# A streaming-encoder layer on eight cores: the second block's attention gate projected ahead of its Q and K, with other staging of the last weights

## The reference, cut to what matters

```python
x = layer_norm(x, ln0_g, ln0_b)
q, k, v, z_a, B, C, h, z_c = split(x @ w_in, 8)        # each 512 wide
y_att  = chunk_attention(q, k, v, rel_bias) * silu(z_a)  # 8 heads of 64, chunks of 64, 8 chunks back
y_conv = B * causal_depthwise_conv3(C * h) * silu(z_c)
hh = concat(y_att, y_conv) @ w_out
out = layer_norm(2 ** 0.25 * x + hh, ln_g, ln_b)
```

## Time and profile before

| what | before |
|---|---|
| median of 3 runs | 1300.98 us (1300.01 to 1301.29) |
| the profiled execution | 1299.6 us, span of its slowest core (core 6) 1298.1 us |
| spans of the cores | 1295.1 (cores 3 and 5) to 1298.1 us (core 6) |
| TensorE busy | 1255.1 us, 97% of the span |
| VectorE, ScalarE, GpSimd busy | 964.7, 742.5, 508.8 us |
| chain that ended last | PE 92%, DMA 3%, issue 2%, DVE 2% |

### The profile page before, as it was taken

How to read it: one execution, slowest core, us unless ns; L and a number is a source line. 1 busy time by engine, 2 the same in 40 slices (tenths; PEclk the granted TensorE clock), 3 DMA queues, 4 the chain that set the end, 5 groups by cost and what they waited for, 6 DMA issues and landing times.

```text
span 1298.1 us, 27186 instructions; the slowest of 8 cores (1295.1 to 1298.1 us)
## 1 busy us (share of the span) xinstructions
PE 1255.1 (97%) x8145; PEld 596.3 (46%) x8308; DVE 964.7 (74%) x1763; ACT 742.5 (57%) x1090; POOL 508.8 (39%) x768
## 2 busy tenths in 40 slices
PE   5989999999999999999999999999999999999996
PEld 3434444444444444444444444444444444444443
DVE  2479976878777686776867768787776867868487
ACT  5775565655536565565654546565564555656562
POOL 2455442533334342443533424434344323424242
PEclk9999999999999999999999999999999999999999
DMA  9993323312233322323213223123232223232022
GB/s 292 324 252 107 88 72 86 90 42 74 72 84 90 82 67 57 83 75 89 74 42 89 75 83 90 47 69 79 78 90 75 73 58 86 74 86 58 10 74 74
DMA packets 125712, 117.15 MB, mean 90 GB/s; under 512 B 103168, under 2 KB 103168, under 8 KB 125440
## 3 DMA queue, kind: packets, MB, share of 16 engines
q1 hardware_dynamic: 125568, 115.40, 32.3%
HBM read 57.69 MB, written 33.55 MB: 70 GB/s over the span
## 4 chain that ended last, share of the span: by engine, by line
PE 92%; DMA 3%; issue 2%; DVE 2%; ACT 1%; SPq 1%; POOL 0%; DVEq 0%; ACTq 0%; POOLq 0%
PE mm L673 32%; PE sc L673 16%; PE mm L684 13%; PE mm L787 12%; PE sc L1015 6%; PE sc L959 5%; PE sc L787 4%; PE sc L684 4%; DMA xs<-w_in 3%; PE sc L856 1%; DVE xs L617 0%; SPq L587 0%; ACT PT L972 0%; DVE xs L926 0%; DVE tz L744 0%
## 5 line engine op out<-in xcount | busy, mean ns | idle before, releaser
L673 PE MATMUL mm<-xnT,w_in_sb 128*128 128x512 bf16 x2002 | 491.9, 379 | 9.3 <-POOL w_in_sb L511 3.8
L972 ACT ACTIVATE PT<-sc 128x1024 bf16<-128x1024 f32 (+1 forms) x288 | 269.9, 1001 | 122.7 <-PE sc L959 121.9
L673 PEld LDWEIGHTS mm<-xnT,w_in_sb 128*128 128x128 bf16 x2072 | 195.3, 98 | 204.8 <-issue 20.1
L673 PE MATMUL sc<-xnT,w_in_sb 128*128 128x512 bf16 x971 | 242.3, 379 | 1.9 <-DVE tz L744 0.6
L1015 PE MATMUL sc<-vA,PT 128*128 128x65 bf16 x2240 | 203.2, 193 | 5.3 <-DVE PT L999 1.8
L1015 PEld LDWEIGHTS sc<-vA,PT 128*128 128x128 bf16 x2240 | 149.3, 97 | 109.3 <-issue 3.5
L1033 POOL TENSOR_TENSOR pvs<-pvs,rden 128x256 f32<-128x256 f32 x128 | 124.6, 974 | 154.6 <-DVE rden L1032 91.3
L999 DVE TENSOR_TENSOR PT<-PT,etab 128x512 bf16<-128x512 bf16 (+1 forms) x304 | 119.9, 404 | 87.4 <-ACT PT L972 83.3
L684 PE MATMUL mm<-w_in_sb,xnT 128*128 128x512 bf16 x745 | 180.5, 379 | 1.2 <-issue 0.6
L787 PE MATMUL mm<-w_out_sb,yT 128*128 128x512 bf16 x695 | 170.4, 379 | 1.3 <-DVE xs L793 0.3
L673 PEld LDWEIGHTS sc<-xnT,w_in_sb 128*128 128x128 bf16 x1000 | 94.0, 98 | 102.5 <-issue 7.8
(11 more groups left out here) (111 smaller groups left out, 1474.1 us busy)
## 6 DMA issues: line engine op xcount, KB each, us to landing
xs<-x SPq DMA_DIRECT2D x64, 512.0 KB, 5.0
out<-xs SPq DMA_DIRECT2D x62, 512.0 KB, 3.3
xs<-w_in SPq DMA_DIRECT2D x20, 512.0 KB, 12.7
g1bc_sb<-w_in SPq DMA_DIRECT2D x4, 512.0 KB, 13.1
b1bc_sb<-w_in SPq DMA_DIRECT2D x4, 512.0 KB, 14.7
vA<-w_in SPq DMA_DIRECT2D x4, 512.0 KB, 13.8
yT<-ytok SPq DMA_TRANSPOSE x128, 2.3
xnT<-rtab SPq DMA_DIRECT2D x1, 1024.0 KB, 15.2
```

Source lines behind the costliest of these rows:

```text
L673: P.op("pe", lambda e, i=i, kc=kc: e.matmul(mm[i][:, :], lhsT=w_in_sb[:, kc, c0:c0 + 128], rhs=xnT[:, sl, kc, :], start=(kc == 0), stop=(k ...
L972: P.op("act", lambda e, x=x, sp=sp, w=w: e.activation(out=PT[:, sp, :, 0:w], in_=sc[x][:, :, 0:w], func=AF.Exp, scale=0.125), reads=scr[x] ...
```

## The change

What the diff does, part by part: (1) block 0 projects the second block's gate ahead of its Q and K; (2) the affine of the second block is done in 16 operations of 128x256, each of which waits for two transposes and not for four, and matmuls wait for the half that they read; (3) the last 12 pieces of `w_in` use `ag0` and `ab0` as two more staging buffers, and both tables are named behind all of `w_in`; (4) all loads of the start but `rtab` and the tables are linked, so that each has a latest time before that of the next (`chain`); (5) a DMA transpose adds 7.6 us per megabyte to the planner's backlog (1.9 us for a tile of the second block); (6) `etab` is tracked per head, and its zeros are written in four pieces; (7) L926 is no longer recorded as a reader of `xhb`; (8) `slow` keeps its generators, so that an `id` is not used again.

```diff
+TR_MB = 7.6
+CHAIN = True
...
+        link = 1e9
         for k in range(len(nodes) - 1, -1, -1):
             n = nodes[k]
...
             n["alap"] -= n.get("early", 0.0)
+            if n.get("chain"):
+                n["alap"] = min(n["alap"], link)
+                link = n["alap"] - n["mb"] / DMA_MB
...
-                dmaq = max(dmaq, s + 0.15) - n["mb"] * 1.2 / DMA_MB
+                dmaq = max(dmaq, s + 0.15) - n["mb"] * TR_MB
...
-                reads=xn1 + ["nrc"], writes=["etab"], us=t_act(256, 1))
-        P.op("pool", lambda e: e.memset(etab[64:128, :, 0:64], 0.0), writes=["etab"], us=0.5)
+                reads=xn1 + ["nrc"], writes=["etab%d" % h], us=t_act(256, 1))
+            if h % 2:
+                P.op("pool", lambda e, h=h: e.memset(etab[64:128, h - 1:h + 1, 0:64], 0.0),
+                     writes=["etab%d" % (h - 1), "etab%d" % h], us=0.2)
...
             if n == 20:
-                bufs = stage[4:]
+                bufs = stage[4:] + [(ag0[:], ["ag0"]), (ab0[:], ["ab0"])]
             if n == 24:
                 if nblk > 1:
                     for t in range(TPB):
                         load_tile(1, t)
-                load_tab(ag0, g0bc_d, "ag0", True)
-                load_tab(ab0, b0bc_d, "ab0", True)
+                        P.nodes[-1]["chain"] = CHAIN
             cast_w(bufs, w_in_d[u], w_in_sb[:, :, u * 128:(u + 1) * 128], "w_in%d" % u)
+        bufs = stage[4:]
+        load_tab(ag0, g0bc_d, "ag0", True)
+        load_tab(ab0, b0bc_d, "ab0", True)
...
-    def second_affine(kc):
+    def second_affine(kc, h):
+        v = xnT[:, 1, kc, 256 * h:256 * h + 256]
         P.op("dve", lambda e: e.tensor_scalar(
-            out=xnT[:, 1, kc, :], in0=xnT[:, 1, kc, :], scalar1=g0T[:, kc:kc + 1], scalar2=b0T[:, kc:kc + 1],
-            op0=ALU.mult, op1=ALU.add),
-            reads=["cst"] + ["xnT1_%d" % t for t in range(TPB)], writes=["xnT1k%d" % kc], us=0.4)
-        P.nodes[-1]["early"] = 6.0 - 0.4 * kc
+            out=v, in0=v, scalar1=g0T[:, kc:kc + 1], scalar2=b0T[:, kc:kc + 1], op0=ALU.mult, op1=ALU.add),
+            reads=["cst"] + ["xnT1_%d" % t for t in (2 * h, 2 * h + 1)], writes=["xnT1k%dh%d" % (kc, h)], us=0.24)
+        P.nodes[-1]["early"] = 1.6 - 0.2 * kc
...
-                reads=yr + ["rstd1_%d" % t, "b1bc", "xs%d" % s, "xhb%d" % (t % 2)], writes=[nm], us=1.28 / wide_ + 0.05 * wide_)
+                reads=yr + ["rstd1_%d" % t, "b1bc", "xs%d" % s], writes=[nm], us=1.28 / wide_ + 0.05 * wide_)
...
-    slow = set()
+    slow = {}
 
     def gated(g):
-        slow.add(id(g))
+        slow[id(g)] = g
         return g
...
-            units += conv[0] + conv[1] + conv[2] + conv[3] + qk[0] + qk[1] + qk[2] + za + qk[3]
+            units += conv[0] + conv[1] + conv[2] + conv[3] + za + qk[0] + qk[1] + qk[2] + qk[3]
```

13 lines of the change are left out of this document (9 added, 4 removed).

## The result

The changed kernel takes 1307.72 us (median of five runs, 1306.65 to 1309.03) against 1300.98: a ratio of 1.006 with a 95% interval of 1.0048 to 1.0071. By the medians it is 6.7 us slower; a ratio of 1.006 would be 7.8. The forecast was 1296.3 us, with a range up to 1302.0, so both the sign and the size were wrong. The profiled execution took 1306.65 us; its slowest core is core 1, with a span of 1305.1 us.

The account below looks back on a forecast made before the run. TensorE was taken to bound fifteen of sixteen blocks, late weights to stall the start. Terms -5.6 + 1.7 - 0.5 - 0.3 = -4.7 us took 1301.0 to 1296.3 us, range 1292 to 1302.

Parts of the forecast that it names:

- The step that failed: All blocks: dearer transposes in the plan, the bias table per head and kept generators cost and give nothing; 0 us.
- The allowance of 0.2 us a block: Later blocks: if the edits taken as free went wrong, 0.2 us in each of fifteen blocks, 3 us.
- the first term: Start: the last `w_in` load goes out ahead of the transposes, so weight wait, clock loss and affine wait go; -5.6 us.
- -5.6 + 1.7 - 0.5: Start: earlier last weights -5.6 us, new stall at the gate units +1.7, shorter attention wait -0.5.
- My list of what can stop the units behind conv group 3: Start, gate units: three possible stops, `tz`, the affine and the transposes; together a stall of 0 to 2.9 us.
- The clock's 1.6 us: Start, after the 3.8 us weight wait: granted clock at 0.50 for 3.2 us, a loss of 1.6 us expected to go.
- The stall at the gates: Start, gate units behind conv group 3: a new stall of 0 to 2.9 us, taken as 1.7, near the transposes alone.
- Rival A: Start: VectorE and `tz` at their worst, stall 4 to 6 us, clock may drop again; 1299 to 1301 us; chance 0.15.
- The split affine: Second block's affine on VectorE: sixteen half-size operations take 2.69 to 5.4 us, taken as 3.5, against 2.69 for eight.
- The wait of attention: Start: TensorE's 1.8 us wait for an attention bias product, fewer gates competing on VectorE; 0 to -1.8, taken as -0.5 us.
- The tail: End: the 4.44 us wait at tile 2's sum of squares for an L926 falls away; -0.3 us, at most -1.4.
- Rival B: Start: residual tables behind the last weights leave VectorE standing and later stop TensorE over 7.3 us; slower; chance 0.12.

Follow-up runs that it names:

- e6: Changed kernel with latest times of the transposes of tiles 2 and 3 in later blocks 3.0 and 1.5 us earlier; 1304.9 us.
- e1: Kernel before with only the planner's higher price of a DMA transpose (7.6 us per MB); 1301.53 us.
- e3: Changed kernel with the planner's old price of a DMA transpose; 1301.76 us.
- e8: Kernel before with only the weights' parts: linked latest times, two more staging buffers, tables behind `w_in`; 1307.98 us.
- e5: Changed kernel with sixty small matmuls added while TensorE is idle at the start, plan otherwise the same; 1306.58 us.
- e7: Changed kernel with the second block's gate units writing their tanh to `tz2` and not `tz`; 1304.24 us.
- e9: Changed kernel without the second block's affine, so the output is not the reference's; 1303.4 us.
- e10: Changed kernel with the affine wide again (eight operations that wait for all four tiles), gate still first; 1301.84 us.
- e11: Kernel before with only the last normalization's wait for `xhb` removed; 1300.81 us.
- e4: Changed kernel with block 0's old order of units, Q and K of three pairs ahead of the gate; 1305.92 us.
- e15: Changed kernel without the second block's affine and with its gates' tanh in `tz2`; output not the reference's; 1304.89 us.
- e12: Kernel before with the higher transpose price, transposes of tiles 2 and 3 due 3.0 and 1.5 us earlier, and generators kept; 1302.12 us.

## Why the prediction was wrong

The start was forecast at -4.4 us and came at +0.2, the middle at 0 and came at +6.0, the tail at -0.3 and came at +0.3: 4.6 + 6.0 + 0.6 = 11.2 of the 11.4 us between forecast and result.

**The step that failed, worth 6.0 us,** is the sentence that the dearer transposes "cost and give nothing that I can find: they move work on engines with room, behind a TensorE that is 99% busy". That TensorE is full says what a block costs when its inputs are on time; it doesn't say with how much to spare they are. I had never read how long before the first Q its last transpose goes out (4.0 us in most blocks before, 3.5 after) and how long it takes to land (3.1 to 3.4 us before, up to 5.3 after). A changed plan is an edit to every block. e6 shows that a margin takes away 4.5 us of the 6.0, e1 that the price alone is enough to bring waits into the kernel before, and e3 that without it most of the loss is gone. But e8 has the same middle at the old price, and e5 moves the late landings with no change of plan, so it is the thin margin that cost the time, and which blocks pay is partly chance: in the kernel before no landing was late. The remaining 1.5 us are other waits (1.3 us on core 1 of e6). The allowance of 0.2 us a block was half the size, and it was put into the range and not into a rival.

**The second step, worth 4.6 us, is the first term.** It happened and gained nothing. The weight wait went, 3.8 us as predicted, by the queue order predicted. But "-5.6 + 1.7 - 0.5" at the start measured +0.2, because a wait removed was answered by waits that I hadn't priced: 1.5 us for the bank of the B unit, `pvs` 2.1, `gate` 0.6 on core 1. e8 is the term by itself, and it is +2.8, with 4.6 us at that bank. My list of what can stop the units behind conv group 3 asked who frees `tz` and who frees the first gate's bank, and not who frees the bank that the first unit takes. That is the B unit's multiply. In the kernel before it (L744) ran at 77.36 us on core 6, ahead of the affine at 83.46; after (L758), it stands behind three operations of the affine. In e8 it stands behind the whole affine, and that waits for the transposes.

**The clock's 1.6 us** was given back too. Read by the granted clock from 62 to 114 us, before, two of eight cores (0 and 5) show no fall, and their first output unit comes at 111.6 and 111.8 us; core 3 has a fall but only 4.1 us of waits, and comes at 111.5; the other five come at 113.9 to 114.3. Waits and the time lost to the clock add up to 5.8 to 6.3 us on the first three and 8.2 to 9.8 us on the five, so the term was sized rightly. Over the eight cores the median of this sum is 8.3 us before and 8.4 after. After, two cores (3 and 5) again show no fall, but these have the longest waits (7.6 and 8.1 us) and reach the mark at 113.7 and 114.3. On core 1 the fall came after waits of 0.8 and 1.5 us, where before it had come after one of 3.8 us.

**The stall at the gates,** 1.7 us from the transposes: the place was right, the releaser was not. The 1.49 us at 80.74 are the bank of the B unit, in no line of the prediction. What I did have, the tanh behind the closing multiply through `tz`, was called just in time with a tanh at 82.2; it ran at 86.66, since the chain took VectorE until 86.23, and TensorE paid for it as the 1.30 us for `pvs` (0.4 in e7). So 1.7 was near the first of these alone, by luck. Rival A had this mechanism, at 4 to 6 us, with 0.15; it would have put the whole at 1299 to 1301.

**The split affine** took 5.0 us for 3.5, near the bound of 5.4 for a cost by instruction. In a row of eight the operations took 2.13 / 8 = 0.27 us each at 128x256, against 2.69 / 8 = 0.34 at 128x512; the rest is that they were scattered. The Trainium skill (VectorE: DVE Perf Modes, The TRN2 errata) was right to speak against it, and by more than the estimate from its figures, 3.6 us. But e9 shows that the whole affine is hidden: without it the start is 0.2 us shorter. Its place, not its size, counts, and then little (e10).

**The wait of attention** was 1.8 us on core 6 before and after: 0 for -0.5, too little to matter. **The tail,** -0.3, measured +0.3, and +0.9 for the edit alone (e11): taking a wait away gave the planner another order, not a shorter one. **Rival B,** late residual tables, did not occur (VectorE waits for no table in after or e8), and the slower side came by a way that had no rival. **Gate before Q and K** is worth 2.6 us inside the new kernel (e4), more than I gave it.

What stays open: what bounds the start. Over all fifteen runs it is 112.7 to 116.8 us while waits for weight, banks and affine come and go. From 62 to 114 us TensorE loses 4 to 10 us to waits on every core. Neither VectorE's 5 us (e9: -0.2) nor the `tz` buffer (e7: +0.7) bounds it alone, and both together give 1.5 us (e15). In e15 the landing of the second block's transposes is next, and e8 waits for it through VectorE; no run brought these transposes forward, so that they bound the start was not tested. The newly planned order differs in each run, so single edits can't be told from it more finely than about 1 us. Why the zeros of `PT` come late in e12 on cores 4 to 7 alone is open too.

## What to carry to other kernels

When an order is planned by costs, an edit to a cost, a due time or a dependence is an edit to every block: list for each transfer in the steady stage how long before its use it is issued and how long it takes to land, and predict those distances before the waits. A bound stage with 99% busy says nothing of that margin, and 0.3 us beside a landing that varies by 1 to 2 us is none. When a wait is removed, ask of the next units who frees the buffer that each of them takes, and what stands ahead of that instruction in its engine's fixed order; in e8 an idle VectorE held TensorE for 4.6 us. And price the removed wait at what the second wait leaves, which you find by removing the one alone: here 4 us of wait were worth nothing.

## What the hardware showed that I had not expected

The landing of a 128x1024 DMA transpose varies with what runs beside it. Over the seventeen traces, eight cores each, the transpose of tile 3 in the later blocks landed in 3.03 to 3.36 us in all 994 cases without a packet on the instruction queues (q8 16 KB, q14 8 KB each) beside the pair. In 908 cases there was one. Of these 727 still took under 4 us and 181 took 4.0 to 5.5 us, though in the stretch shown such packets are about 1% of the engines' time. In the kernel after, a packet on q8 beside the pair went with 4.25 us or more in 16 cases of 16; in the kernel before, ten such cases took 3.4 us at most, and where within the landing the packet falls seems to count. Adding 60 instructions at the start of TensorE's program moved the late landings to other blocks and brought the sum of the waits over the cores from 33.5 to 20.2 us (e5). Code that does no work in a stage can so set which of its transfers are late.
